# A decoder layer with 32 experts: expert weights in four homes of 4 MB, interleaved halves, and the gather written transposed

## The reference, cut to what matters

```python
xt = rmsnorm(x, ln2)                       # 264 rows of 1024
logits = xt @ w_router + b_router          # 32 experts
top_v, top_i = lax.top_k(logits, 4); gate = softmax(top_v)
# for each expert e, over the rows that chose it:
gu = xb @ w_gate_up[e] + b_gate_up[e]      # 1024 x 2048
gt, up = gu[..., :1024], gu[..., 1024:]
act = (clip(up, -7, 7) + 1) * (min(gt, 7) * sigmoid(1.702 * min(gt, 7)))
y = act @ w_down[e] + b_down[e]            # 1024 x 1024
out[token] += gate * y
```

## Time and profile before

| | us |
|---|---|
| three runs | 1394.49, 1383.91, 1392.07 |
| median | 1392.07 |
| profiled execution, its own time | 1394.99 |
| span of its instructions | 1393.2 |

### The profile page before, as it was taken

One profiled execution on the slowest core, in us unless ns is written; L12 is line 12 of the kernel. 1 busy time (PEld: TensorE's weight loads), 2 busy tenths in 40 slices (PEclk: granted clock), 3 DMA queues, 4 the chain that ended last, 5 costly groups with the idle time before them and its releaser, 6 DMA issues.

```text
span 1393.2 us, 16949 instructions
## 1 busy us (share of the span) xinstructions
PE 1316.5 (94%) x6704; PEld 627.8 (45%) x6704; DVE 377.2 (27%) x705; ACT 259.2 (19%) x473; POOL 79.6 (6%) x48
## 2 busy tenths in 40 slices
PE   6999969798889999999999999999999999999996
PEld 5888846797745333333333333333333333333332
DVE  3043765975453211111112111121112111121112
ACT  2113433122202111111111111121111111111112
POOL 0000151360000000000000000000000000000001
PEclk9999978898897899999999999999999999999998
DMA  8356673013458699999999999999999999999994
GB/s 263 133 158 166 227 210 79 4 44 124 156 188 341 247 415 428 429 428 429 428 429 428 429 429 429 429 429 428 429 429 429 429 428 429 428 429 428 429 429 168
DMA packets 52505, 459.93 MB, mean 330 GB/s; under 512 B 7922, under 2 KB 10300, under 8 KB 27884
## 3 DMA queue, kind: packets, MB, share of 16 engines
q1 hardware_dynamic: 49252, 451.45, 78.6%
q0 software_dynamic: 1888, 5.34, 2.0%
q10 hardware_dynamic: 1328, 2.64, 0.6%
HBM read 454.27 MB, written 5.11 MB: 330 GB/s over the span
## 4 chain that ended last, share of the span: by engine, by line
PE 83%; DMA 6%; DVE 4%; issue 3%; ACT 2%; POOL 1%; SPq 1%; ACTq 0%; DVEq 0%; POOLq 0%
PE ps L1688 30%; PE ps L1715 15%; PE ps L1290 8%; PE ps L1651 4%; PE ps L1636 4%; PE ps L1673 4%; PE ps L1421 3%; DMA work<-in_w_gate_up 2%; DMA ring<-in_w_gate_up 2%; PE ps L1549 2%; PE ps L1265 2%; PE ps L1643 2%; ACT work L703 1%; DVE ring L826 1%; PE ps L1490 1%
## 5 line engine op out<-in xcount | busy, mean ns | idle before, releaser
L1688 PE MATMUL ps<-ring,work 128*64 128x512 f32 x1536 | 338.5, 596 | 2.5 <-DMA ring<-in_w_gate_up 1.6
L1688 PEld LDWEIGHTS ps<-ring,work 128*64 128x64 f32 x1536 | 108.3, 137 | 229.3 <-issue 225.1
L1715 PE MATMUL ps<-ring,work 128*64 128x512 f32 x768 | 170.1, 595 | 0.0
L1290 PE MATMUL ps<-work,ring 128*128 128x264 f32 x672 | 152.0, 389 | 0.4 <-DVE work L826 0.4
L1200 DVE TENSOR_SCALAR work<-ps 128x512 f32<-128x512 f32 x32 | 22.2, 692 | 437.1 <-PE ps L1688 437.1
L1290 PEld LDWEIGHTS ps<-work,ring 128*128 128x128 f32 x672 | 128.6, 192 | 22.7 <-DVE work L826 0.5
L1218 DVE SCALAR_TENSOR_TENSOR work<-work 128x512 f32<-128x512 f32 x32 | 24.1, 752 | 348.1 <-ACT work L735 348.1
L1688 PE MATMUL ps<-work 128*64 128x512 f32 x512 | 113.2, 594 | 0.5 <-DMA work<-in_w_gate_up 0.5
L1715 PEld LDWEIGHTS ps<-ring,work 128*64 128x64 f32 x768 | 53.0, 137 | 115.4 <-issue 115.4
L726 ACT ACTIVATE work<-work 128x512 f32<-128x512 f32 x32 | 20.2, 632 | 442.6 <-DVE work L1200 442.6
L826 DVE TENSOR_TENSOR work<-work 128x512 f32<-128x512 f32 (+8 forms) x79 | 62.4, 790 | 52.7 <-ACT work L518 46.7
(11 more groups left out here) (263 smaller groups left out, 1086.6 us busy)
## 6 DMA issues: line engine op xcount, KB each, us to landing
ring<-in_w_gate_up SPq DMA_DIRECT2D x96, 2048.0 KB, 21.5
ring<-in_w_down SPq DMA_DIRECT2D x48, 2048.0 KB, 25.7
work<-in_w_gate_up SPq DMA_DIRECT2D x32, 2048.0 KB, 22.2
work<-in_w_down SPq DMA_DIRECT2D x16, 2048.0 KB, 26.3
ring<-in_w_in SPq DMA_DIRECT2D x6, 3072.0 KB, 15.8
ring<-in_w_out SPq DMA_DIRECT2D x1, 4096.0 KB, 14.3
ring<-in_w_in SPq DMA_DIRECT2D x2, 1536.0 KB, 8.7
ring<-in_cache_k SPq DMA_DIRECT2D x16, 192.0 KB, 3.3
```

The costliest lines, as they stand in the source:

```text
L1290: last = mm(psum(job, T), WIN[gi % 2][:, k, j * 128:(j + 1) * 128], hT[:, k, :], start=k == 0, stop=k == KD - 1)
L1688: last = mm(PS[bnk][g * 64:g * 64 + 64, :], lhs, UNIT[n % 8][:, w0 + base + g * 512:w0 + base + (g + 1) * 512], start=False, stop=k == KD - 1)
L1715: last = mm(PS[BY][g * 64:g * 64 + 64, :], lhs, UNIT[n % 8][:, w0:w0 + 512], start=k == 0, stop=k == KD - 1)
```

## The change

- A unit is now 4 MB, 32 KB in each partition: gate and up are two units (four steps k each), down is one. There are four homes, unit n in home n mod 4, so still 16 MB. Row p*4+j (gate and up) and p*8+j (down) of the weights lies in partition p.
- Two units an iteration of four experts come in two DMAs of 2 MB, 16 KB a partition: n = 4, whose first half is asked for after k = 1 of the first expert of the four (`half_used`), and n = 11, the w_down of the fourth, whose first half has a semaphore of its own.
- `unit_used` is raised after k = 3 and k = 7, and once after the whole w_down. Ahead of the stage the homes are given free as 1, 2 and 1.
- Halves: g = 0 takes columns 0-3, 8-11, 16-19 and so on, g = 1 takes 4-7, 12-15 and so on. The moving operand of gate, up and the biases so has runs of four elements, with four left out between them. A step c of w_down still reads `up[:, c:512:4]`.
- The gather writes its result transposed: `h2` (every fourth column) is the stationary operand, `sel` of two experts (128 slots) the moving one, eight matmuls of 128x128 by 128x128 for a half of the width. One half is done in each expert, into `XG[0]` or `XG[1]` for the next pair. `gather_T`, its four transposes, and the ACT copy to `xg` are gone. VectorE makes four `sel` at once, in every first expert of a pair.
- The product is transposed and copied before `selg`. All four bias matmuls stand after w_down; none is left ahead of it.
- Ahead of the first expert: `open_sum` is taken apart, one matmul earlier, one later; two gathers instead of one; VectorE adds the samples' bias before the gates.
- Small tiles move to where two of the old homes were.

```diff
-        UNIT = [view(RING, 4096 * 5, 4096), ..., view(RING, 4096, 4096)]
+        UNIT = [view(RING, 8192 * 2, 8192), view(RING, 8192, 8192), view(WORK, 20408, 8192), view(RING, 0, 8192)]
...
+                        if u < 2:
+                            src = wgu[bass.ds(first + j, 1), u * 512:(u + 1) * 512, :].rearrange("a (p j) n -> p (a j n)", j=4)
                         else:
+                            src = wdn[bass.ds(first + j, 1)].rearrange("a (p j) n -> p (a j n)", j=8)
+                        if n == 4:
+                            sp.wait_ge(S_("half_used"), turn4 + 1)
+                            sp.dma_start(unit[:, 0:4096], src[:, 0:4096]).then_inc(S_("ld_half"), 16)
+                        elif n == 11:
+                            sp.wait_ge(S_("unit_used"), it * 3 + n + 1)
+                            sp.dma_start(unit[:, 0:4096], src[:, 0:4096]).then_inc(S_("ld_down_half"), 16)
+                        sp.wait_ge(S_("unit_used"), it * 3 + n + 1)
+                        rest = slice(4096 if n in (4, 11) else 0, 8192)
+                        sp.dma_start(unit[:, rest], src[:, rest]).then_inc(done, 16)
...
-            def gather(sem_name, count):
-                pe.wait_ge(S_(sem_name), count)
-                for m in range(2):
-                    for g in range(2):
-                        last = mm(PS[BX][g * 64:g * 64 + 64, :], sel[:, m, :], h2[:, m, g * 512:(g + 1) * 512],
-                                  start=m == 0, stop=m == 1)
+            def gather(half):
+                for c in range(4):
+                    for m in range(2):
+                        last = mm(PS[BX][:, c * 128:(c + 1) * 128], h2[:, m, half * 512 + c:(half + 1) * 512:4],
+                                  sel[:, m].rearrange("p e s -> p (e s)"), start=m == 0, stop=m == 1)
                 last.then_inc(S_("xg_full"), 1)
...
+            def split(rows, g):
+                return rows.rearrange("q (p g j) -> q g p j", g=2, j=4)[:, g]
...
-                for g in range(2):
+                for i, g in ((0, 0), (1, 1), (0, 1), (1, 0)):
                     q = slice(i * NE, (i + 1) * NE)
-                    mm(PS[(BG, BU)[i]][g * 64:g * 64 + 64, :], pick[q, :], ebias[q, g * 512:(g + 1) * 512], start=True, stop=False)
+                    mm(PS[(BG, BU)[i]][g * 64:g * 64 + 64, :], pick[q, :], split(ebias[q, :], g), start=True, stop=False)
...
                     for bnk, base in ((BG, 0), (BU, 1024)):
                         for g in range(2):
                             last = mm(PS[bnk][g * 64:g * 64 + 64, :], lhs,
-                                      UNIT[n % 8][:, w0 + base + g * 512:w0 + base + (g + 1) * 512], start=False, stop=k == KD - 1)
-                    if k % 2:
+                                      split(UNIT[n % 4][:, w0 + base:w0 + base + 1024], g), start=False, stop=k == KD - 1)
+                    if k == 1 and j == 0:
+                        last.then_inc(S_("half_used"), 1)
+                    if k % 4 == 3:
                         last.then_inc(S_("unit_used"), 1)
                 combine(it)
-                gather("sel_next", it * 2 + 2)
+                if j % 2 == 0:
+                    pe.wait_ge(S_("sel_next"), it * 2 + 4)
+                pe.wait_ge(S_("xgT_out"), it + 2)
+                gather(j % 2)
+                pe.wait_ge(S_("act"), it + 1)
+                for c in range(4):
+                    last = nc.tensor.transpose(PS[BG][:, c * 128:(c + 1) * 128], up[:, c:512:4], C["ident"])
+                last.then_inc(S_("actT_full"), 1)
                 pe.wait_ge(S_("selg"), it * 2 + 2)
...
-                gather_T(it + 1)
...
-                bias(1, it + 2)
                 pe.wait_ge(S_("selgT_out"), it + 2)
                 pe.wait_ge(S_("actT_out"), it + 1)
...
-                bias(0, it + 2)
+                bias(it + 2)
```

More of the change, by code:

```diff
@@ L296, in build @@
         rexp = place(NM, NE)
-        sel = place(2, SLOT)
+        sel = place(2, 2, SLOT)
         selgT = place(256)
@@ L722, in _ @@
             with act.Fori(0, passes) as p:
[L723 to L735, removed]
+                with act.Fori(0, NE // 4) as q:
+                    for j in range(4):
+                        it = act.snap(p * NE + q * 4 + j)
+                        act.wait_ge(S_("gt"), it + 1)
+                        nc.scalar.activation(sg, gt, ACT.Sigmoid, scale=ALPHA).then_inc(S_("sg"), 1)
+                        gathered(j // 2 + 1, j % 2, it + 3)
+                        act.wait_ge(S_("actT_full"), it + 1)
+                        nc.scalar.activation(actT, PS[BG][:, :].rearrange("p (c s) -> p c s", c=4), ACT.Copy).then_inc(S_("actT_out"), 1)
+                        act.wait_ge(S_("selgT_full"), it + 1)
+                        nc.scalar.activation(selgT, PS[BY][:, 0:256], ACT.Copy).then_inc(S_("selgT_out"), 1)
+                        act.wait_ge(S_("samp_out"), it + 1)
+                        act.wait_ge(S_("unit_used"), it * 3 + 7)
+                        nc.scalar.activation(yS, PS[BY][:, :], ACT.Copy).then_inc(S_("y_out"), 1)
             A_(nc.scalar.activation(lss[:1], eps[:1], ACT.Sqrt))
@@ L1173, in _ @@
                 V(v.scalar_tensor_tensor(posx[:, m, 0:NE], psum("rk", 3, NE)[:, m, :], 1.0, selr[:, m, :], ALU.add, ALU.mult))
-            for m in range(2):
-                ins = v.tensor_scalar(sel[:, m, :], C["slots"][:, 0:SLOT], posx[:, m, 0:1], None, ALU.is_equal)
-                V.ready(ins, "sel", 1) if m == 1 else V(ins)
+            for n in range(4):
+                m, e_ = n // 2, n % 2
+                ins = v.tensor_scalar(sel[:, m, e_, :], C["slots"][:, 0:SLOT], posx[:, m, e_:e_ + 1], None, ALU.is_equal)
+                V.ready(ins, "sel", 1) if n == 3 else V(ins)
             V.free(v.tensor_reduce(mcount, psum("rk", 3, NE)[:, 2, :], AX.X, ALU.max), "rk")
@@ L1560, in h2_T @@
                 for g in range(2):
-                    transposes(f"ht{m}{g}", [half(h2[:ROWS[m], m, :], 2 * g + c // 2, c % 2) for c in range(4)], ROWS[m])
+                    transposes(f"ht{m}{g}", [h2[:ROWS[m], m, g * 512 + c:(g + 1) * 512:4] for c in range(4)], ROWS[m])
             def logits(m):
@@ L1611, in _ @@
             last.then_inc(S_("gate_s_full"), 1)
-            open_sum(0)
             give("rk")
@@ L1656, in _ @@
             pe.wait_ge(S_("ld_ebias"), 32)
-            bias(0, 1)
-            bias(1, 1)
-            gather_T(0)
+            bias(1)
+            pe.wait_ge(S_("xgT_out"), 1)
+            gather(1)
             pe.wait_ge(S_("gate"), 3)
-            pe.wait_ge(S_("xgT_out"), 1)
+            pe.wait_ge(S_("samp_out"), 1)
             for m in range(2):
-                last = nc.tensor.transpose(PS[BX][0:NE, m * 128:(m + 1) * 128], gate[:, m, :], C["ident"])
+                last = nc.tensor.transpose(PS[BY][0:NE, m * 128:(m + 1) * 128], gate[:, m, :], C["ident"])
             last.then_inc(S_("gateT_full"), 1)
```

180 lines of the change are left out of this document (86 added, 94 removed).

## The result

| | before | after |
|---|---|---|
| median of four runs, us | 1389.52 | 1412.81 |
| lowest to highest | 1383.91 to 1394.49 | 1412.64 to 1413.57 |
| span of the profiled execution | 1393.2 | 1410.6 |
| first expert's start to the end of the last w_down | 460.2 to 1379.8: 919.6 | 457.9 to 1397.2: 939.3 |

The ratio is 1.016, interval 1.013 to 1.019: slower by 1.6%, where 0.1% was forecast, and outside the range. The table's last line already has all of it. So I compare kernels by **the stage**, from the first expert's start to the end of the last w_down: 939.3 against 919.6 us, 19.7 more.

What follows compares the result with a forecast made beforehand. The weight transfer at 428 GB/s was taken as the limit (29.4 us an expert, 0.8 more than TensorE needs). Start +1.4, breaks +2.5, rate -5.3, end +2.2 and last combine +0.9 made +1.7: 1393.8 us, range 1380 to 1405.

Steps and rivals of the forecast that it cites:

- the gather's term in step 4: TensorE's work in an expert: 16 gather instructions take 1.70 to 1.95 us, where 1.89 was.
- 28.5 + 0.23 = 28.73: TensorE's forecast mean time an expert, 28.5 us, plus its slack of 0.23 us an expert before it decides.
- Rate: Expert weight stream: 32 KB packets halve the fixed part per byte, -5.3 us, bounds 0 and -12.7.
- The other estimate of part 1: Packet gain in the weight stream by the Trainium skill's fixed overhead of about 3 cycles: 0.3%, 2.2 us.
- Gaps in the moving operand: Gate and up reads in runs of four: taken as costing nothing; rival at 15%, 1452 us, chance 0.08.
- The middle: From gate/up's end to w_down in an expert: 5.85 us, in the second of a pair 5.57; before 6.72.
- The rival in which TensorE becomes the bound by its middle: Uncovered ACT copies between gate/up and w_down: 29.0 to 29.2 us an expert, 11 later, 1405 us; chance 0.13.
- Biases: Four bias matmuls in a row after w_down, two at a time: 1.9 us.
- Breaks: Gaps in the weight stream waiting for free homes: 3.6 us against 1.1 before, +2.5, bounds 0 and +5.
- Start: Ahead of the first expert: open_sum taken apart, second gather, gather_T gone: +1.4 us, bounds -1 and +2.5.
- The end: TensorE's work behind the last landing it waits for: 19.6 us where 17.4 stood, +2.2.
- the +0.9 of the last combine: After the last w_down: the last combine comes after four biases, not two, +0.9 us.

Runs made afterwards that it cites:

- e1_plain: The kernel after, with the gather's stationary operand taking 128 adjacent columns of h2 instead of every fourth (gathered rows' order not the reference's); 1382.92 us.
- e4_sorted: The kernel after, with VectorE writing h2 sorted by column mod 4, so gather and h2 transposes read adjacent columns; median 1387.96 us, ratio 0.997 to the kernel before.
- e5_16k: e4_sorted with each unit asked for as two DMAs of 16 KB a partition; median 1395.89 us, ratio 1.003 to the kernel before.
- e6_halves: e4_sorted with units 6 and 10 also loaded in halves; median 1389.41 us, ratio 0.998 to the kernel before.

## Why the prediction was wrong

**The step that failed is the gather's term in step 4.** I had 16 instructions at 0.106 (plain) to 0.122 us (transposes of every fourth column), 1.70 to 1.95, and "15% slower" as the price of the gaps. Measured 0.232 apart and 4.0 in all. The row was of another kind of instruction: a transpose, which reads its operand with a step of four at hardly any cost, here too, in the kernel after. An fp32 matmul of 128 stationary columns had no row with a step, and its bound had to reach to twice the time, as I did allow for the moving operand. A slower kernel had been given a chance of 0.13. Shown by `e1_plain` (one slice changed, 2.00 us, stage 916.0) and the series of steps.

How 2.0 us an expert became 19.7 in all: with plain loads TensorE needs 32 x 27.4 = 877 us and the stage takes 916, as the stream sets its end. So 39 us of TensorE's time are free, 1.2 an expert, and it becomes the bound from 28.6 us an expert on. I had 28.5 + 0.23 = 28.73: the threshold was right, to 0.1. At 29.37 it is exceeded by 0.74, x 32 = 24; measured 939.3 - 915.6 = 23.7 between the kernel after and `e4_sorted`. Against the kernel before, the other parts of the change give 4 us back. The term was too small by 2.1 us and the expert by only 0.9, since the terms of the biases and of the middle (below) were too large by 1.2.

The Trainium skill, SBUF — State Buffer, "Door 1: The DMA port swizzle", says that a new 16-byte line costs. I cited it for just this operand and then took the 15% of the transposes as its size. The series agrees with the rule itself: what counts is the lines touched, 1.8 ns each here, to be seen only once they take longer than the plain load.

**Point by point.**
- *Rate*, -5.3: right; -5.8 by `e5_16k`. The other estimate of part 1, 2.2, was too small. In the kernel after it can't be seen, since TensorE sets the pace. "It is wrong if the rate stays at 428" was said, and it did, but for the other reason named beside it: the chain stayed on TensorE.
- *Gaps in the moving operand*, taken as nothing, 0.08 for the rival: right, 594 ns against 596.
- *The middle*: without the load, 27.53 - 13.91 - 7.09 - 1.02 = 5.5 and 5.3 in `e4_sorted`, where 5.85 and 5.57 stood. The rival in which TensorE becomes the bound by its middle had the right outcome and nearly the right size (29.0 to 29.2 us an expert, 1405), but for another cause: the ACT copies are a chain without cover (18.4 us of TensorE's idle time in the page above), and the sum had already counted it; the 0.5 more is not there. That the outcome matched this rival is luck.
- *Biases*, 1.9: they take 1.02, all four side by side, which was my lower bound. With a plain load, this and the middle give TensorE 27.4, not 28.5.
- *Breaks*, 3.6: 4.0 in the kernel after, 2.2 with plain loads.
- *Start*, +1.4: the first expert starts 2.4 us earlier than before, not later, and the clock is granted in full from 440 to 460 us (1.00; 0.57 in the kernel before). The gather's term was too small here too: the second of the two takes 3.9 us at full clock, and 3.6 had been counted for half clock. The sum also took off 1.6 for `gather_T` and its waits, where its own terms make 1.8. Kernels that differ from this one only in the gather's slice began the stage at 451.7 to 463.4, so one profile can't size this term.
- *The end*: +2.2 is right (19.6 us from the landing, in `e1_plain`), the +0.9 of the last combine is nothing: 13.4 us follow w_down in both kernels, since four biases take 1.02 and two took 1.00.

## What to carry to other kernels

Before a stationary operand is read with a step, count the 16-byte pieces that it touches: in fp32 two elements a piece cost this stage nothing, one a piece doubled the load, and the cure was to let the producer write it sorted, in an operation that was there anyway (0.7 us longer each, three times, against 2.0 us in each of 32 experts). Take a duration only from a row of the same kind of instruction; a transpose doesn't stand for an fp32 matmul, even with the same shape and step. And where two resources are within a few per cent, work out from which duration on the second one decides, and give every term of that sum without a row of its own a bound on the far side of it.

## What the hardware showed that was not expected

- VectorE's write of 128 x 1024 fp32 took 2.00 us with every 256th place in turn, 1.28 in order.
- The load of 128 fp32 stationary columns, by step: 0.111, 0.118, 0.175, 0.232 and 0.237 us apart at steps 1, 2, 3, 4 and 8. Transposes with a step of four stay at 0.12; why they are exempt was not tried.
- Four matmuls with 32 rows and 64 columns of weights, 512 wide, run side by side in 1.02 us (eight instructions), as long as two do (1.00).
- With the gather's moving operand halved, each w_down behind it ran partly at the half clock (granted 0.83 and 8.50 us in the one shown, instead of 7.09), and the kernel became 60 us slower by doing less. In `e6_halves` four stretches of 32 gate and up matmuls ran so too (8.54 to 8.78 us, granted 0.80 to 0.82, the last at 1269.65), each behind a wait of 2.7 us for a landing; a fifth wait of that length (until 918.93) had no such stretch behind it.
